# A decoder layer's MLP: the down projection as one level of Strassen's product in seven of eight blocks of the hidden width

## What is computed

```
x  = x + rms_norm(y @ w_out, norm_g[1])
hm = rms_norm(x, norm_g[2])
y  = square(relu(hm @ w1)) @ w2          # w1: 1024 x 4096, w2: 4096 x 1024
out = x + rms_norm(y, norm_g[3])
```

## Time and profile before

| | |
|---|---|
| median of 3 runs | 656.25 us (655.77 to 657.12) |
| profiled execution, its own time | 656.78 us |
| its span, first to last instruction | 655.0 us |
| TensorE busy | 624.7 us, 95% |
| VectorE, ScalarE, GpSimd busy | 264.9, 251.7, 248.7 us |
| MLP, up tile 0's second half to the last matmul | about 305 to 648.6 us |

### The profile page before, as it was taken

One profiled execution on the slowest core, in us unless ns is written; L12 is line 12 of the kernel. 1 busy time (PEld: TensorE's weight loads), 2 busy tenths in 40 slices (PEclk: granted clock), 3 DMA queues, 4 the chain that ended last, 5 costly groups with the idle time before them and its releaser, 6 DMA issues.

```text
span 655.0 us, 8146 instructions
## 1 busy us (share of the span) xinstructions
PE 624.7 (95%) x3256; PEld 513.6 (78%) x3256; DVE 264.9 (40%) x506; ACT 251.7 (38%) x442; POOL 248.7 (38%) x96
## 2 busy tenths in 40 slices
PE   2999999998898889999999999999999999999995
PEld 2988888886776668879888888888888888888884
DVE  4526031107888884695831023411133210234045
ACT  5415273107578871563551204331134321233211
POOL 4322537202627330034537313555222555052610
PEclk9999999999899999999999999999999999999998
DMA  9442457605311240024234411244303262123002
GB/s 282 122 128 66 129 137 200 160 1 161 111 53 39 53 136 1 0 65 130 83 142 130 129 64 65 67 137 125 120 0 129 65 192 65 64 65 129 1 32 97
DMA packets 49818, 63.49 MB, mean 97 GB/s; under 512 B 6616, under 2 KB 34292, under 8 KB 49780
## 3 DMA queue, kind: packets, MB, share of 16 engines
q1 hardware_dynamic: 49620, 62.71, 31.8%
q10 hardware_dynamic: 160, 0.26, 0.2%
HBM read 58.51 MB, written 2.10 MB: 93 GB/s over the span
## 4 chain that ended last, share of the span: by engine, by line
PE 84%; DVE 8%; ACT 4%; issue 2%; DMA 1%; POOL 1%; SPq 0%; DVEq 0%; ACTq 0%
PE ps L1334 26%; PE ps L1336 26%; PE ps L1335 26%; PE ps L1596 2%; PE ps L1581 1%; ACT W L677 1%; PE ps L1476 1%; DMA raw<-in_w_in 1%; DVE xres L1265 1%; PE ps L1500 1%; DVE stat L1096 1%; DVE probsT L1108 1%; PE ps L1501 1%; DVE stat L1160 1%; PE ps L1353 1%
## 5 line engine op out<-in xcount | busy, mean ns | idle before, releaser
L492 POOL TENSOR_TENSOR ring_l<-raw,ring_h 128x2048 fp32r<-128x2048 f32 (+2 forms) x48 | 215.3, 4492 | 315.2 <-ACT ring_h L561 315.2
L1334 PE MATMUL ps<-xT_h,ring_h 128*128 128x512 f32 (+1 forms) x384 | 143.0, 372 | 0.5 <-DVE xT_l L1237 0.5
L1336 PE MATMUL ps<-xT_h,ring_l 128*128 128x512 f32 (+1 forms) x384 | 143.2, 373 | 0.0
L1335 PE MATMUL ps<-xT_l,ring_h 128*128 128x512 f32 (+1 forms) x384 | 143.0, 373 | 0.0
L561 ACT ACTIVATE ring_h<-raw 128x2048 fp32r<-128x2048 f32 (+1 forms) x48 | 90.3, 1890 | 90.4 <-PE ps L1336 57.9
L1334 PE MATMUL ps<-ring_h,hT_h 128*128 128x512 f32 x256 | 100.9, 394 | 0.0
L1336 PE MATMUL ps<-ring_h,hT_l 128*128 128x512 f32 x256 | 100.8, 394 | 0.0
L1335 PE MATMUL ps<-ring_l,hT_h 128*128 128x512 f32 x256 | 100.6, 393 | 0.0
L1304 DVE TENSOR_TENSOR sq<-relu 128x512 f32<-128x512 f32 x32 | 45.6, 1426 | 103.4 <-ACT relu L845 103.4
L1334 PEld LDWEIGHTS ps<-xT_h,ring_h 128*128 128x128 f32 x384 | 72.6, 189 | 13.5 <-DVE xT_l L1237 0.8
L1335 PEld LDWEIGHTS ps<-xT_l,ring_h 128*128 128x128 f32 x384 | 72.4, 188 | 12.6
(11 more groups left out here) (222 smaller groups left out, 660.3 us busy)
## 6 DMA issues: line engine op xcount, KB each, us to landing
raw<-in_w_mlp SPq DMA_DIRECT2D x32, 1024.0 KB, 5.3
raw<-in_w_in SPq DMA_DIRECT2D x9, 1024.0 KB, 5.3
raw<-in_nsa_cmp_w SPq DMA_DIRECT2D x8, 512.0 KB, 7.1
xres<-in_x SPq DMA_DIRECT2D x4, 512.0 KB, 5.5
raw<-in_w_out SPq DMA_DIRECT2D x2, 1024.0 KB, 6.5
raw<-in_w_out SPq DMA_DIRECT2D x4, 512.0 KB, 4.2
out<-xres SPq DMA_DIRECT2D x8, 256.0 KB, 2.1
gain_a<-in_norm_g SPq DMA_DIRECT2D x3, 512.0 KB, 5.9
```

The lines of the kernel that those rows point to most:

```text
L492: nc.gpsimd.tensor_tensor(ring_l[r][:, n0:n], raw[c % RAW][:, n0:n], ring_h[r][:, n0:n].bitcast(F32), ALU.subtract).then_inc(lo_done, 1)
L1334: nc.tensor.matmul(o, sh, mh, start=start, stop=False)
L1335: nc.tensor.matmul(o, sh, ml, start=False, stop=False)
L1336: return nc.tensor.matmul(o, sl, mh, start=False, stop=stop)
```

## The change

**The product.** The MLP becomes eight blocks (NB) of four hidden tiles (FB = 4). In blocks 0 to 6 the down projection of a block (512 tokens x 512 hidden by 512 hidden x 1024) is cut into 2 x 2: the squares into A11, A12, A21, A22 (rows: 256 tokens, columns: 256 hidden, index q counts the two hidden tiles of a part), the weights into B11, B12, B21, B22 (256 hidden x 512 outputs). Strassen's product in the form with running sums takes seven products of parts in place of eight. It needs four sums of squares, S1 = A21 + A22, S2 = S1 - A11, S3 = A11 - A21, S4 = A12 - S2, and four of weights, B12 - B11, B22 minus that, B22 - B12, B21 minus the second. Each product is two token tiles (s) x two hidden tiles (q) x three matmuls. Products 0, 2, 4, 6 share the banks 2 and 3, products 1, 3, 5 the banks 4 and 5: within a pair of banks the next product goes on in the same accumulation (except product 5, which starts fresh), so that a bank holds a running sum which VectorE adds to `y` after each product.

**Buffers.** The squares of four hidden tiles' worth of tokens lie in `sq`; of the eight 256-column parts of it (`sq[:, j]`), 0 to 3 are one pair of hidden tiles, 4 to 7 their four sums. ScalarE squares the relu in place. The high and low halves of parts 1 to 7 are one instruction each of 7 x 256 = 1792 columns (`a_high`, `a_low`), one pair of hidden tiles (q) at a time. The ring is now cut into slots of 1024 columns, eight in all: an up tile is one slot, a product's weights are one slot. w2 goes to its own buffer `raw_d`, a block of 2 MB in two transfers; the sums of weights go into `sum0` and into the buffer of `gain_a`. The low halves of the slots that come from weight sums (products 1, 2, 4, 6) are VectorE's, the others GpSimd's.

**Order.** The up tiles run two ahead: before block b's products come the up tiles to 4b+5 (all 32 before block 6's). Block 7 is computed as before, in three matmuls per product, but with both halves of the outputs for a token tile one after the other, in two chains per tile, added to `y` once each, with `finish(t)` after both. The loads of the MLP leave the chunk scheme for `load_up` and `load_down`.

```diff
-FB = 8
+FB = 4
 NB = FF // P // FB
...
+TH, LAST = SEQ // 2, NB - 1
+PRODUCTS = [(0, 2, True), (3, 4, True), (4, 2, False), (6, 4, False), (5, 2, False), (2, 4, True), (1, 2, False)]
+ADDS_TO = [(2, 0), (0, 1), (2, 1), (2, 1), (0, 1), (2, 0), (0, 0)]
+ADDED_BEFORE = [5 - 7, 4 - 7, 3 - 7, 2, 1, 0, 6 - 7]
+SUM_SLOTS = [1, 2, 4, 6]
+PER_STRASSEN = 2 * len(PRODUCTS)
+LAST_BANK = [(0, 1), (6, 7), (4, 5), (2, 3)]
+def mlp_slots():
+    slots = [("up", f) for f in range(6)]
+    for b in range(LAST):
+        slots += [("down", b, k) for k in range(7)]
+        if b < LAST - 2:
+            slots += [("up", f) for f in range(4 * b + 6, 4 * b + 10)]
+        elif b == LAST - 2:
+            slots += [("up", f) for f in range(4 * b + 6, 4 * NB)]
+    return slots + [("down", LAST, j) for j in range(4)]
...
+        def slot_free(n):
+            if n < 8:
+                return released(C_WO + n // 2)
+            s = SLOTS[n - 8]
+            return (up_done, s[1] + 1) if s[0] == "up" else (down_done, PER_STRASSEN * s[1] + 2 * (s[2] + 1))
...
+            def load_up(q):
+                if q < 2:
+                    sp.wait_ge(lo_done, split_no(C_MLP - 2 + q) + 1)
+                else:
+                    for j in range(2):
+                        sp.wait_ge(*slot_low(SLOT["up", 2 * (q - 2) + j]))
...
+            def load_down(b):
+                if b == 0:
+                    sp.wait_ge(hmt_done, 2 * NT)
+                else:
+                    sp.wait_ge(*slot_low(SLOT["down", b - 1, 5]))
+                    sp.wait_ge(*slot_low(SLOT["down", b - 1, 4]))
+                    sp.wait_ge(sum_ready, 4 * b)
...
+            load_up(2)
+            load_down(0)
+            for b in range(1, LAST):
+                load_up(2 * b + 1)
+                load_up(2 * b + 2)
+                load_down(b)
...
-            for c in range(C_MLP, NCHUNK):
-                low_half(c)
+            for n in POOL_SLOTS:
+                pool.wait_ge(hi_done, SLOT0 + n + 1)
+                nc.gpsimd.tensor_tensor(slot(ring_l, n), slot_source(n), slot(ring_h, n).bitcast(F32),
+                                        ALU.subtract).then_inc(lo_done, 1)
...
+            def slot_high(n):
+                act.wait_ge(*slot_loaded(n))
+                act.wait_ge(*slot_free(n))
+                nc.scalar.activation(slot(ring_h, n), slot_source(n), ACT.Copy).then_inc(hi_done, 1)
...
                     if t == NT - 1 and half == 0:
-                        high_half(C_MLP + 1)
+                        slot_high(2)
+                        slot_high(3)
...
+            def relu_squared(f):
+                j = f % 4 if f >= FB * LAST else f % 2
+                tile = sq[:, 2 * j:2 * j + 2, :].rearrange("p a t -> p (a t)")
+                act.wait_ge(up_done, f + 1)
+                if f >= 2:
+                    act.wait_ge(al_ready, min(f // 2, 2 * LAST))
+                nc.scalar.activation(tile, ps[:, UP_BANK[f % 4], :], ACT.Relu).then_inc(relu_ready, 1)
+                act.wait_ge(relu_ready, f + 1)
+                nc.scalar.activation(tile, tile, ACT.Square).then_inc(sq_ready, 1)
+            def a_high(q):
+                act.wait_ge(s_ready, q + 1)
+                if q >= 2 and q % 2 == 0:
+                    act.wait_ge(down_done, PER_STRASSEN * (q // 2))
+                nc.scalar.activation(a_h[:, q % 2], sq[:, 1:8, :], ACT.Copy).then_inc(ah_ready, 1)
...
+            relu_squared(0)
+            relu_squared(1)
+            a_high(0)
+            down_high(0, 0)
+            relu_squared(2)
+            relu_squared(3)
+            down_high(0, 1)
+            a_high(1)
+            down_high(0, 2)
+            down_high(0, 3)
+            relu_squared(4)
+            down_high(0, 4)
+            down_high(0, 5)
+            relu_squared(5)
+            down_high(0, 6)
+            for b in range(1, LAST):
+                if b < LAST - 1:
+                    for f in range(4 * b + 2, 4 * b + 6):
+                        slot_high(SLOT["up", f])
+                    for k in range(3):
+                        down_high(b, k)
+                    a_high(2 * b)
+                    down_high(b, 3)
+                    relu_squared(4 * b + 2)
+                    down_high(b, 4)
+                    relu_squared(4 * b + 3)
+                    down_high(b, 5)
+                    a_high(2 * b + 1)
+                    relu_squared(4 * b + 4)
+                    down_high(b, 6)
+                    relu_squared(4 * b + 5)
...
+            def a_sums(q):
+                dve.wait_ge(sq_ready, 2 * q + 2)
+                a21, a11, a22, a12, s1, s2, s3, s4 = (sq[:, j, :] for j in range(8))
+                link(nc.vector.tensor_tensor(s1, a21, a22, ALU.add))
+                link(nc.vector.tensor_tensor(s2, s1, a11, ALU.subtract))
+                nc.vector.tensor_tensor(s3, a11, a21, ALU.subtract)
+                nc.vector.tensor_tensor(s4, a12, s2, ALU.subtract).then_inc(s_ready, 1)
+            def a_low(q):
+                dve.wait_ge(ah_ready, q + 1)
+                nc.vector.tensor_tensor(a_l[:, q % 2], sq[:, 1:8, :], a_h[:, q % 2].bitcast(F32), ALU.subtract).then_inc(al_ready, 1)
...
+            def add_product(b, k, s):
+                n = PER_STRASSEN * b + 2 * k + s
+                t, half = ADDS_TO[k]
+                ya = y[:, t + s, 512 * half:512 * half + 512]
+                dve.wait_ge(down_done, n + 1)
...
+            a_sums(0)
+            a_low(0)
+            for k in range(3):
+                b_sum(0, k)
+            b_sum_low(0, 0)
+            a_sums(1)
+            a_low(1)
+            b_sum_low(0, 1)
+            b_sum_low(0, 2)
+            b_sum(0, 3)
+            b_sum_low(0, 3)
+            a_sums(2)
+            for b in range(LAST):
+                if 1 <= b < LAST - 1:
+                    b_sum_low(b, 0)
+                    b_sum_low(b, 1)
+                    a_low(2 * b)
+                    b_sum_low(b, 2)
+                    b_sum(b, 3)
+                    a_sums(2 * b + 1)
+                    a_low(2 * b + 1)
+                    b_sum_low(b, 3)
+                    a_sums(2 * b + 2)
...
+                for k in range(7):
+                    for s in range(2):
+                        add_product(b, k, s)
+                    if b < LAST - 1 and 3 <= k < 6:
+                        b_sum(b + 1, k - 3)
...
+            def product(b, k, s, wh, wl):
+                a, bank, fresh = PRODUCTS[k]
+                before = PER_STRASSEN * b + 2 * (k - 2 if k >= 2 else (6 if k == 0 else 5) - 7) + s
+                if before >= 0:
+                    pe.wait_ge(acc_ready, before + 1)
+                o = ps[:, bank + s, :]
+                for q in range(2):
+                    ah, al = a_h[:, q, a, P * s:P * s + P], a_l[:, q, a, P * s:P * s + P]
+                    go_on = {} if fresh else {"skip_group_check": True}
+                    nc.tensor.matmul(o, ah, wh[:, q, :], start=fresh and q == 0, stop=not fresh, **go_on)
+                    nc.tensor.matmul(o, ah, wl[:, q, :], start=False, stop=not fresh, **go_on)
+                    last = nc.tensor.matmul(o, al, wh[:, q, :], start=False, stop=not fresh or q == 1, **go_on)
+                last.then_inc(down_done, 1)
+            def down(b):
+                pe.wait_ge(al_ready, 2 * b + 2)
+                for k in range(7):
+                    wh, wl = mlp_slot(SLOT["down", b, k])
+                    for s in range(2):
+                        product(b, k, s, wh, wl)
...
+            for f in range(6):
+                up(f)
+            for b in range(LAST):
+                if b == LAST - 1:
+                    up(4 * b + 6)
+                    up(4 * b + 7)
+                down(b)
+                if b < LAST - 1:
+                    for f in range(4 * b + 6, 4 * b + 10):
+                        up(f)
+            down_last()
```

More of the change, by code:

```diff
@@ L87, with by_sums @@
 EARLY_F, EARLY_T = 4, 2
-SETS = [(0, 1, 6, 7), (2, 3, 4, 5)]
+UP_BANK = (0, 1, 6, 7)
+TH, LAST = SEQ // 2, NB - 1
[14 more added lines that the diff above has]
+    return slots + [("down", LAST, j) for j in range(4)]
+SLOTS = mlp_slots()
+SLOT = {s: n for n, s in enumerate(SLOTS)}
+SLOT0 = C_MLP - (C_WO - C_CMP)
+def by_sums(n):
+    return SLOTS[n][0] == "down" and SLOTS[n][1] < LAST and SLOTS[n][2] in SUM_SLOTS
+POOL_SLOTS = [n for n in range(1, len(SLOTS)) if not by_sums(n)]
+SUMS = [n for n in range(len(SLOTS)) if by_sums(n)]
 def ring_slot(c):
@@ new lines, in _ @@
+            load_up(0)
+            sp.wait_ge(s_done, 2 * NU)
+            sp.dma_start(gain_b[:], norm_g[0, 2:3, :].to_broadcast([P, D])).then_inc(gain2_in, 16)
+            load_up(1)
+            load_up(2)
[4 more added lines that the diff above has]
+                load_down(b)
+            load_up(2 * LAST + 1)
+            load_down(LAST)
+            sp.wait_ge(*slot_low(SLOT["down", LAST - 1, 2]))
@@ new lines, in b_sum @@
+            def b_sum(b, k):
```

(51 more changed lines are left out.)

327 lines of the change are left out of this document (149 added, 178 removed).

## The result

The changed kernel takes **663.81 us** (median of 4 runs, 663.45 to 664.97), the kernel before 656.60 on the same chip: ratio 1.0114, 95% interval 1.0097 to 1.0132. The change costs 7.2 us, where +12.6 was forecast. The profiled execution of after has 664.02 us around a span of 662.3, against the span of 655.0 before. TensorE saved what it should and then lost more than that by waiting.

The account below looks back on a forecast made before the run. TensorE, busy 95% of the span, was taken to bound the kernel. The terms -19.4 + 2.4 + 2.7 + 15.0 + 1.7 + 10.0 + 0.2 = +12.6 us gave 669 us, range for 8 in 10: 647 to 677.

Parts of the forecast that it names:

- (c): Block 0, from A, the end of the second squares' low half: product 2 waits 15.0 us for the first addition.
- (e): Blocks 1 to 5, from T, the end of the previous block's products: product 2 waits 2.0 us, five times, 10.0.
- (a): Before the MLP: GpSimd's earlier split gets between VectorE's multiplies, TensorE's transposes wait; 2.4 us, bounds 0 and 4.8.
- tail: After the last matmul: the 6.6 us chain stays, two small VectorE operations more at the last tile, +0.2 us.
- The gain: Down projection of seven blocks: 84 matmuls fewer at 0.231 us each, -19.4 us.
- (b): Start of block 0: TensorE waits 2.7 us for the squares' low half, 0.3 without the GpSimd turn.
- (d): After block 0's long wait: 3.4 us of matmuls at half clock cost 1.7 us, bounds 0 and 3.4.
- (f): Weight loads of the MLP: the same megabytes, landed before they are needed, cost nothing.
- the port does not stack: Rival: waiting VectorE operations pass together or are blocked less than a split long; 641 to 645 us; chance 0.22 (641 to 653).
- Only block 0 suffers: Rival: the middle blocks' fourth square sum slips in, 10.0 becomes 1.5; +4.1, 660 us; chance 0.25.
- The clock oscillates: Rival: TensorE pauses of 2.0 us in each block bring half clock each time; 678 us; chance 0.07.
- GpSimd serves its queue first: Rival: in the middle blocks the last square sum waits two splits more, 5 x 4.8; 693 us; chance 0.04.

Follow-up runs that it names:

- e4: The changed kernel with product 6 of each Strassen block accumulated twice, 84 matmuls more, output not the layer's: 683.74 us.
- e3: The changed kernel with GpSimd's splits of slots 2 and 4 held until VectorE's normalising multiplies of tiles 2 and 3 are done: 660.23 us.
- e2: The changed kernel with ScalarE splitting the weights of up tiles 6 to 9 only after block 0's first addition: 659.69 us.
- e9: The changed kernel with 46 matmuls into an unused bank in place of TensorE's long wait in block 0: 663.33 us.
- e10: The changed kernel with each GpSimd low half of an MLP slot in two instructions of 512 columns instead of one of 1024: 653.95 us.
- e1: The changed kernel with the next block's square sums, in blocks 0 to 5, spread behind the additions of products 0, 1 and 2: 657.41 us.
- e5: e7 plus e3's two waits of GpSimd: 646.24 us, 0.984 of the kernel before.
- e8: e6 with block 0's product 2 additions ahead of its last low half and block 1's square sums after products 4 to 6: 642.51 us.
- e11: e8 with the low halves of GpSimd's MLP slots in two instructions of 512 columns each, as in e10: 639.68 us.
- e7: The changed kernel with VectorE reordered: block 0's additions earlier, its square sums later, the middle blocks' fourth sum behind product 0's additions: 651.25 us.
- e6: e5 with two of the three weight sums at block 0's start moved from ahead of a_low(1) to behind it: 643.44 us.

## Why the prediction was right or wrong

The direction and the mechanism stand: VectorE's operations with two SBUF inputs wait for GpSimd's splits in turns, and product 2 of block 0 pays for it. The sizes are off in both directions, and they cancel in part: (c) and (e) were taken 8.9 us too large, (a), the second stretch at half clock and the tail 4.3 too small. That 663.8 lies well inside the stated range owes something to this and to the range's width, 30 us.

- *The gain*, -19.4: confirmed by e4, at 0.233 to 0.237 instead of 0.231 a matmul, so -19.6 to -19.9.
- *(a) handover*, taken 2.4, measured 4.8, the upper bound, from tile 2's pair of multiplies to the first relu; against the start of the span it is 4.0. The pair of tile 2 took 3.51 instead of 1.42, held by one GpSimd split, the pair of tile 3 5.78, held by two; the first relu came 4.0 us later although the pair began 0.7 earlier than in the earlier trace rows. e3 shows what the term left out: of 4.8, 3.1 were waits and some 1.7 the clock's fall, which step (d) had reserved for the long wait. e3 took all 4.8 away between these two points. "Some comes back by a shorter split later" did not happen.
- *(b) start of block 0*, 2.7: measured 2.5. It also brought the clock down ("once more at b"): TensorE ran at half clock from 336.1 to 339.5, so products 0 and 1 came 1.7 us late. This cost nothing of its own, since product 2 had to wait anyway.
- *(c) block 0*, product 2 forecast at A+20.4, came at 353.31, which is A+18.7. The chain took its five turns as written: two ahead of the last low half, which ended at A+10.2 (10.8 forecast), and three among the four sums. These took 7.9 and not 8.9, since a held sum is 2.4 to 2.6 in all, where its own 0.43 had been put on top of the 2.4. The wait itself, 11.3 instead of 15.0, is shorter by that 1.7, and by the 1.7 that products 0 and 1 were late. e2 shows 6.2 of it to be three turns. Without any turn the estimate was 4.0; e2, with two turns left in the chain, has 5.1.
- *(d) clock*, 1.7: after the long wait half clock for 3.3 us of work, 1.6 lost; e9 got 1.4 of it back between product 2 and block 1's first wait. The size was not fixed by the kernel: behind the same product's wait e3 and e10 lost 2.4 and e2 3.0, all inside the bounds of 0 and 3.4. The falls were three, not one; the other two are counted in (a) and (b).
- *(e) middle blocks*, 5 x 2.0: this term failed. The fourth sum did wait a turn (2.64, the trace above), as forecast and as the Trainium skill has it ("SBUF — State Buffer", "Who interferes with whom": the one issued first goes, for its whole instruction). But TensorE waited 0.6 to 0.9 and not 2.0, in all 3.5 as listed and 4.8 between starts (e10), where 10.0 was forecast. The chain stood about 1 us earlier: the additions of the previous block ended 0.7 us after its last product (369.0), where 1.4 was taken, and the fourth sum ended at T+27.4, where 28.6 was taken. One microsecond decided 5 us of the sum, because it came five times. e10 shows that the 3.5 is the turn: with halves it is gone.
- *(f) loads*: nothing, as forecast; 5.4 and 6.0 us to landing in the page, and TensorE waited for no load.
- *Tail*: 7.8 us from the last matmul to the end of the span, 6.6 before, against +0.2. VectorE's part is 4.2 in both, so the two small operations cost nothing to speak of. The rest divides the runs cleanly: all that keep the order of the square sums have 7.7 or 7.8 (after, e2, e3, e4, e9, e10), all that move them 6.7 or 6.8 (e1, e5 to e8, e11). In the traces of the first group one packet of 8 KB on the queue that the page calls "instruction" starts 5.9 to 6.1 us after the last matmul, and SyncE's last branch comes at 7.3 to 7.4; in the second group it starts at 3.0 to 4.1, before the last stores have landed, and the branch comes at 6.3 to 6.5. In the kernel before there is no such packet near the end, and the branch comes at 6.3. So 1.1 us of the change's cost, and of every reordering's gain, most likely hangs on when this packet comes; no run moved it by itself.

The profile closes when every term is taken between starts of matmuls, and with e4's price of the matmuls: -19.9 + 4.0 + 2.7 + 1.7 + 11.4 + 1.6 + 4.8 + 1.2 = +7.5 (+7.8 with 19.6), against 662.3 - 655.0 = +7.3.

Of the rivals, *the port does not stack* is refuted by the four sums above. *Only block 0 suffers* (660, own range 656 to 664) was nearer to the time than the forecast, though not by its reason: the fourth sum did not slip in. *The clock oscillates* did not occur: the clock was 1.00 from 360 to 600 us through all five waits of under 1 us. Its condition, pauses of 2.0 us, did not come about either, so it was not tested as stated. *GpSimd serves its queue first* is refuted by the same four lines, which alternate with its splits.

## What to carry to other kernels

Removing matmuls from a kernel that TensorE bounds is worth their full issue period, but the adds that replace them must be placed: count them against the engine pair that excludes each other, and put every operation that frees a PSUM bank ahead of everything that is not due yet. If two engines take turns at a shared resource, the length of the other engine's instruction is the price of every turn, so cut that engine's instructions before you reorder anything: here five lines brought 9.9 us, and the order together with e3's two waits another 14, of which 1.1 is the tail. After each repair look at where the wait went; nearly every reordering here gave part of its gain back behind the next operation in the same queue.

## What the runs showed of the hardware

- Splitting GpSimd's instructions cost GpSimd 251.2 to 280.0 us of busy time, and VectorE's went from 419.9 down to 396.2. The waiting is counted as busy in the page (a sum of 0.42 us of work is listed with 2.4 to 2.6), so the busy share does not tell of this contention; the duration of a small operation does.
- The turns are strict. With work queued on both sides, each VectorE operation (0.42 us by itself) let exactly one GpSimd instruction pass: 2.4 to 2.6 us with 1024 columns, 1.37 to 1.49 with 512. A sum that came while a split was half done waited for the rest of it alone (1.31 us, e1). The additions out of PSUM were never held: all 98 of the changed kernel took 0.67 to 0.69 us, many beside running splits.
- The clock fell at nearly every single wait of 2.1 to 2.6 us (at both in the changed kernel, at all three in e7, in e6 and e8 at the one there was), but in e5 it stayed full through waits of 2.4 and 2.8. So the length of a wait did not decide it alone. It did not fall after waits of up to 1.2 in the middle of matmuls. In the halved version a wait of only 1.03 at the normalisation still brought half clock; TensorE had been busy for 0.92 of the 2 us from 290 there. At half rate it stayed 3.4 us after the waits of up to 3.5, 6.8 over the 5.1 of e2, 10.2 over the 11.3 of the changed kernel and the 8.3 of e10, and 13.7 over the 11.5 of e3; of these 3.3 to 6.1 us fell on work behind the long wait.
